# Moving the low parts of split weights from VectorE to GpSimd in a two-layer mLSTM/GLA decoder step

## The chip, the core and the metric

The kernel runs on one core of a Trainium2 chip. The metric is the device time of one execution in microseconds; the time before is the median of three runs. TensorE is the matmul engine, VectorE, ScalarE and GpSimd are the engines for elementwise work, SyncE issues the DMAs.

## The reference

1024 prompt tokens and 64 sample tokens (8 sequences of 8) go through two layers. Each layer is a token mixer (layer 0 an mLSTM, layer 1 gated linear attention, GLA) and a SwiGLU feed-forward, each between two RMS norms:

```
for i in range(2):
    h = rms_norm(x, g_pre_mix[i])
    mix = mlstm(h) if i == 0 else gla(h)        # in-projection, chunked recurrence, out-projection
    x = x + rms_norm(mix, g_post_mix[i])
    h = rms_norm(x, g_pre_ffn[i])
    h = (silu(h @ w_gate[i]) * (h @ w_up[i])) @ w_down[i]
    x = x + rms_norm(h, g_post_ffn[i])
```

D_MODEL is 1024, the feed-forward is 2816 wide, all data is fp32. The states of both mixers are outputs too.

## The kernel before, in words

Activations lie transposed, features on the 128 partitions and tokens along the columns, in two blocks: block 0 has 512 tokens, block 1 has 576, as two halves of 288.

**Split matmuls.** A product in fp32 is made of three products in the faster fp32r type. Every weight tile and every activation tile has a high part (its value in fp32r) and a low part (what is left), and TensorE adds low x high, high x high and high x low in PSUM (`products`, line 813).

**Units.** The work of TensorE on weights is a list of 396 units, each with one weight tile of 128 x 1024: P (a 128-column piece of an in-projection), W (out-projection), G and U (gate and up), D (two pieces of the down-projection, four groups of 128 outputs each). In the feed-forward they come as G D D U G U, over and over. A unit takes 24 matmuls of 512 columns in block 0 or 48 of 288 in block 1. The unit of number n uses slot n mod 3 of three buffers: `w_stage` (as loaded), `w_hi`, `w_lo`.

**Who makes what for unit n.** SyncE loads `w_stage` (line 567); it waits until the low part of the unit three before is made (semaphore `w_lo`). ScalarE makes `w_hi` by a copy that rounds (line 1079), after TensorE has left the slot. VectorE makes `w_lo = w_stage - w_hi` (`lo`, line 1363) after a wait on `w_hi`, and TensorE starts the unit after a wait on `w_lo`.

**Order.** Each engine runs the list of units in its own program, written out by loops: for unit n first the parts of unit n + 2 (ScalarE `hi`, VectorE `lo`), then its eviction, then the steps that tags have put beside that unit. VectorE puts `lo(n + 2)` ahead of the eviction, in a D unit between the first and the second group:

```
for q, grp in enumerate(u.groups):
    if q == 1 and n + 2 < len(units):
        lo(n + 2)
```

Evictions: a G tile is evicted by ScalarE (line 1132, `evicted`). A U tile is multiplied with it by VectorE (line 1391), ScalarE copies the product to `hid_hi` (line 1136), VectorE makes `hid_lo` (line 1394). A D group is copied to Y (line 1405, first pair) or added to it (line 1407) by VectorE; TensorE has four PSUM banks for all units and waits until a bank has been emptied.

**Steps beside the units.** A norm is a rstd (lines 1424 to 1429, after sums of squares, line 1374, and a matmul with a matrix of means, line 849), then the rows of the post norm, two to a unit (lines 1439 and 1442, then the squares), then the rows of the next pre norm (line 1458 for the value, ScalarE's high part, line 1454 for the low part). They stand beside units of the other block that are not D. The mixers' chunks of 128 tokens are spread over units in the same way; of the GLA's, `la1` and `la2` make exponents of seven levels (lines 1650, 1651) and the decayed keys (line 1691), for which TensorE waits at line 950.

GpSimd has four memsets of constants before the program, and no part in it.

Of the kernel before, what the change touches and what calls it, by code (L numbers as in the profile page):

```python
# [7 lines left out]
F32 = mybir.dt.float32  # L8
F32R = mybir.dt.float32r
U32 = mybir.dt.uint32  # L10
ALU = mybir.AluOpType
# [3 lines left out]
D = 1024  # L15
# [33 lines left out]
NW = 3  # L49
# [285 lines left out]
def wait(eng, sem, value):  # L335

    if value > 0:
        eng.wait_ge(sem, value)
# [131 lines left out]
def program(nc, g, plan, a):  # L470
    units, norms = plan.units, plan.norms
    s = {name: nc.alloc_semaphore(name) for name in SEMS}
# [13 lines left out]
    def grouped(ap, blk):  # L486
        return ap.rearrange("p (g t) -> p g t", g=NG[blk])

    def bank(b, blk):
        return ps[:, b:b + NG[blk], 0:GW[blk]]  # L490
# [51 lines left out]
    def unit(kind, layer, blk, i, j=0):  # L542
        return units[plan.at[kind, layer, blk, i, j]]

    rstds_before = {}
    n = 1
# [14 lines left out]
    with nc.Block() as block:  # L561
# [505 lines left out]
        def _(act):  # L1067
# [283 lines left out]
            for n, u in enumerate(units):  # L1351
# [3 lines left out]
                for t in u.tags:  # L1355
                    if t[0] in steps:
                        steps[t[0]](*t[1:])

        @block.vector
        def _(dve):  # L1360
            def lo(n):
                dve.wait_ge(s["w_hi"], n + 1)
                dve.tensor_tensor(g.wlo[:, n % NW, :], g.wst[:, n % NW, :], g.whi[:, n % NW, :].bitcast(F32),  # L1363
                                  ALU.subtract).then_inc(s["w_lo"], 1)

            def add_square(i, k, b):
                j = SUM(i, k)
                acc, sq = g.n.acc[:, 0:NT[b]], g.n.sq[:, j % 2, 0:NT[b]]
                dve.wait_ge(s["squared"], j + 1)
                if k == 0:  # L1370
                    dve.tensor_copy(acc, sq).then_inc(s["summed"], 1)
                else:
                    dve.wait_ge(s["summed"], j)
                    dve.tensor_tensor(acc, acc, sq, ALU.add).then_inc(s["summed"], 1)  # L1374

            def evict(n, u):
                b = u.blk
                if u.kind == "P" and u.i >= 17:
                    dve.wait_ge(s["left_act"], u.groups[0].ev)
                    E = g.E[:, u.slot, 0:NT[b]]  # L1380
                    j = V_HEAD[u.layer] + u.i - 17
                    dve.tensor_scalar(E, E, g.vec[:, j:j + 1], None, ALU.mult).then_inc(s["gained"], 1)
                elif u.kind == "W":
                    add_square(plan.norm[2 * u.layer, b].sum0, u.i, b)
                elif u.kind == "U":
                    grp = u.groups[0]
                    pr = g.E[:, 2, 0:NT[b]]
                    dve.wait_ge(s["groups"], grp.n + 1)
                    dve.wait_ge(s["left_act"], unit("G", u.layer, b, u.i).groups[0].ev)
                    wait(dve, s["hid_lo_ready"], u.hid - 1)  # L1390
                    dve.tensor_tensor(grouped(pr, b), bank(grp.bank, b), grouped(g.E[:, u.i % 2, 0:NT[b]], b), ALU.mult  # L1391
                                      ).then_inc(s["left_dve"], 1)
                    dve.wait_ge(s["hid_hi_ready"], u.hid)
                    dve.tensor_tensor(g.hl[:, u.i % 2, 0:NT[b]], pr, g.hh[:, u.i % 2, 0:NT[b]].bitcast(F32),  # L1394
                                      ALU.subtract).then_inc(s["hid_lo_ready"], 1)
                elif u.kind == "D":
                    N = plan.norm[2 * u.layer + 1, b]
                    for q, grp in enumerate(u.groups):
                        if q == 1 and n + 2 < len(units):
                            lo(n + 2)  # L1400
                        m = 4 * u.j + q
                        Y = grouped(g.Y[b][:, m, :], b)
                        dve.wait_ge(s["groups"], grp.n + 1)
                        if u.i == 0:
                            dve.tensor_copy(Y, bank(grp.bank, b)).then_inc(s["left_dve"], 1)
                        else:
                            dve.tensor_tensor(Y, bank(grp.bank, b), Y, ALU.add).then_inc(s["left_dve"], 1)  # L1407
                        if u.i == PAIRS - 1 and q:
                            add_square(N.sum0, m - 1, b)
                    if u.i == PAIRS - 1:  # L1410
                        add_square(N.sum0, 4 * u.j + 3, b)


            def sumx(n, k0, k1):
                for k in range(k0, k1):
                    add_square(norms[n].sum1, k, norms[n].blk)
# [413 lines left out]
                     "mg4": mgates, "ma": ma, "mb": mb, "md": md, "me": me, "lg": lgate, "la1": la1, "la2": la2, "la3": la3,  # L1830
                     "l1": l1, "l2": l2, "lb": lb, "le": le, "ss": ss, "sh": sh}
            dve.wait_ge(s["consts"], 16 * CONSTS)
            lo(0)
            sumx(0, 0, KD)
            lo(1)
            rstd(0, 1)
            pre(0, 0, KD)
            for n, u in enumerate(units):
                if u.kind != "D" and n + 2 < len(units):
                    lo(n + 2)  # L1840
                evict(n, u)
                for t in u.tags:
                    if t[0] in steps:
                        steps[t[0]](*t[1:])
# [93 lines left out]
```

## Time and profile before

| | |
|---|---|
| three runs | 2768.99, 2770.28, 2760.65 us; median 2768.99 us |
| the profiled execution | 2773.79 us, its span 2771.7 us |
| granted TensorE clock, mean | 0.986 |
| TensorE matmuls | 2652.2 us busy (96%), 16042 |
| VectorE | 1489.8 us busy (54%), 2286 instructions |
| ScalarE | 1020.4 us busy (37%), 1455 instructions |
| GpSimd | 0.2 us busy, 4 instructions |
| DMA | 331.25 MB, 120 GB/s |

The span is the time from the first to the last instruction of the profiled execution. The busy time of TensorE's matmuls comes from pipelined instructions with modelled ends, so that 96% busy does not mean 96% of its peak. An idle engine costs time only where another waits for it.

### The profile page before, as it was taken

The page shows a single profiled execution, that of the slowest core. Times are in us where ns is not written, and L with a number is a line of the kernel's source. Part 1 is how long each engine was busy: PE and PEld are TensorE (multiplying, and loading weights), DVE is VectorE, ACT ScalarE, POOL GpSimd, SP SyncE. Part 2 cuts the span into 40 slices and gives each one's busy share as a digit, 9 for nine tenths or more (in the row PEclk, how much of TensorE's full clock was granted, in tenths as well). Part 3 has the DMA queues.
Part 4 walks back from the last instruction along what each step waited for, and adds up shares of the span by engine and source line. Part 5 has one row for each costly group of instructions (what it writes and reads, how often), then busy time and mean ns, then how long its engine had stood idle before and what let it go on. Part 6 is the DMA issues. An engine that isn't in the chain of part 4 may idle for free.

```text
span 2771.7 us, 38345 instructions
## 1 busy us (share of the span) xinstructions
PE 2652.2 (96%) x16042; PEld 2392.2 (86%) x16042; DVE 1489.8 (54%) x2286; ACT 1020.4 (37%) x1455; POOL 0.2 (0%) x4
## 2 busy tenths in 40 slices
PE   5999999999999999999999999999999989999996
PEld 3889998877987998789999987998886979999996
DVE  4534455555367663356655676326766377444435
ACT  3443344542334332344433343325343243222222
POOL 0000000000000000000000000000000000000000
PEclk9999999999999999999999999999999999999998
DMA  4455445435323332442332333344225433322222
GB/s 159 140 162 156 129 144 157 132 114 173 126 84 127 106 120 100 153 146 74 106 104 69 115 110 121 125 134 139 90 91 182 133 110 126 111 83 85 77 84 84
DMA packets 181728, 331.25 MB, mean 120 GB/s; under 512 B 19477, under 2 KB 98965, under 8 KB 181557
## 3 DMA queue, kind: packets, MB, share of 16 engines
q1 hardware_dynamic: 181556, 328.81, 36.8%
q8 instruction: 127, 2.08, 0.3%
q14 instruction: 45, 0.36, 0.0%
HBM read 272.48 MB, written 56.28 MB: 119 GB/s over the span
## 4 chain that ended last, share of the span: by engine, by line
PE 83%; DVE 9%; ACT 4%; issue 2%; DMA 2%; SPq 0%; ACTq 0%; DVEq 0%
PE ps L813 75%; PE ps L967 2%; ACT w_hi L1079 1%; DMA w_stage<-w_down_in 1%; DVE Y L1439 1%; DVE n_xs L1442 1%; DVE w_lo L1363 1%; DVE evicted L1391 1%; ACT hid_hi L1136 1%; DVE n_normed L1458 1%; PE ps L908 1%; PE ps L901 1%; PE ps L1042 1%; PE ps L902 1%; PE ps L993 0%
## 5 line engine op out<-in xcount | busy, mean ns | idle before, releaser
L813 PE MATMUL ps<-HH,w_lo 128*128 128x288 f32 (+1 forms) x3696 | 1026.0, 332 | 10.1 <-DVE HL L1454 7.4
L813 PE MATMUL ps<-HH,w_hi 128*128 128x288 f32 (+1 forms) x3696 | 1012.1, 328 | 0.0
L813 PE MATMUL ps<-HL,w_hi 128*128 128x288 f32 (+1 forms) x3696 | 1012.1, 328 | 0.0
L813 PEld LDWEIGHTS ps<-HH,w_lo 128*128 128x128 f32 x3696 | 632.3, 189 | 74.3 <-issue 17.9
L1363 DVE TENSOR_TENSOR w_lo<-w_stage,w_hi 128x1024 fp32r<-128x1024 f32 x396 | 483.8, 1222 | 358.4 <-ACT w_hi L1079 357.5
L813 PEld LDWEIGHTS ps<-HL,w_hi 128*128 128x128 f32 x3696 | 631.1, 189 | 49.5
L813 PEld LDWEIGHTS ps<-HH,w_hi 128*128 128x128 f32 x3696 | 631.2, 189 | 47.3
L1079 ACT ACTIVATE w_hi<-w_stage 128x1024 fp32r<-128x1024 f32 x396 | 416.2, 1052 | 474.9 <-PE ps L813 347.4
L813 PE MATMUL ps<-hid_hi,w_lo 128*128 128x288 f32 (+1 forms) x1056 | 300.8, 340 | 37.9 <-DVE Y L1407 18.0
L1407 DVE TENSOR_TENSOR Y<-ps,Y 128x512 f32<-128x512 f32 (+1 forms) x320 | 227.5, 721 | 153.8 <-PE ps L813 153.0
L813 PE MATMUL ps<-hid_lo,w_hi 128*128 128x288 f32 (+1 forms) x1056 | 293.0, 332 | 0.0
L813 PE MATMUL ps<-hid_hi,w_hi 128*128 128x288 f32 (+1 forms) x1056 | 293.0, 332 | 0.0
L813 PEld LDWEIGHTS ps<-hid_hi,w_lo 128*128 128x128 f32 x1056 | 183.1, 193 | 64.8 <-issue 21.9
L1136 ACT ACTIVATE hid_hi<-evicted 128x512 fp32r<-128x512 f32 (+1 forms) x88 | 57.9, 658 | 430.2 <-DVE evicted L1391 430.2
L813 PEld LDWEIGHTS ps<-hid_lo,w_hi 128*128 128x128 f32 x1056 | 183.6, 193 | 15.0
L813 PEld LDWEIGHTS ps<-hid_hi,w_hi 128*128 128x128 f32 x1056 | 183.5, 193 | 13.5
L1391 DVE TENSOR_TENSOR evicted<-ps,evicted 128x512 f32<-128x512 f32 (+1 forms) x88 | 63.6, 723 | 209.5 <-PE ps L813 209.5
L1105 ACT ACTIVATE evicted<-ps 128x512 f32<-128x512 f32 (+1 forms) x96 | 59.9, 624 | 281.5 <-PE ps L813 281.4
L1374 DVE TENSOR_TENSOR n_sum<-n_sum,n_sq 128x512 f32<-128x512 f32 (+1 forms) x112 | 80.9, 723 | 99.7 <-ACT n_sq L1085 96.1
L1132 ACT ACTIVATE evicted<-ps 128x512 f32<-128x512 f32 (+1 forms) x88 | 54.8, 623 | 174.4 <-PE ps L813 174.1
L1394 DVE TENSOR_TENSOR hid_lo<-evicted,hid_hi 128x512 fp32r<-128x512 f32 (+1 forms) x88 | 63.9, 726 | 63.7 <-ACT hid_hi L1136 63.7
L1085 ACT ACTIVATE n_sq<-n_xs 128x512 f32<-128x512 f32 (+1 forms) x64 | 41.6, 657 | 70.5 <-DVE n_xs L1442 69.0
(191 smaller groups left out, 1618.2 us busy)
## 6 DMA issues: line engine op xcount, KB each, us to landing
w_stage<-w_in_in SPq DMA_DIRECT2D x100, 512.0 KB, 3.7
w_stage<-w_gate_in SPq DMA_DIRECT2D x88, 512.0 KB, 3.5
w_stage<-w_up_in SPq DMA_DIRECT2D x88, 512.0 KB, 3.6
w_stage<-w_down_in SPq DMA_DIRECT2D x88, 512.0 KB, 3.6
w_stage<-w_out_in SPq DMA_DIRECT2D x32, 512.0 KB, 4.1
proj_scratch<-evicted SPq DMA_DIRECT2D x48, 288.0 KB, 2.2
proj_scratch<-evicted SPq DMA_DIRECT2D x48, 256.0 KB, 2.1
x_scratch<-n_xs SPq DMA_DIRECT2D x3, 2304.0 KB, 9.3
```

The lines of the kernel that those rows point to most:

```text
L813: mm = pe.matmul(ps[:, grp.bank + t, 0:W], wsl(w, k), x[:, k, t * W:(t + 1) * W], start=(q == 0 and m == 0), stop=(q == len(ks) - 1 and m ...
L967: mm = pe.matmul(ps[0:n, M0 + b, at + h * m:at + (h + 1) * m], k, q, start=True, stop=True)
L1079: act.activation(g.whi[:, n % NW, :], g.wst[:, n % NW, :], ACT.Copy).then_inc(s["w_hi"], 1)
L1085: act.activation(grouped(dst, b) if src.shape != dst.shape else dst, src, ACT.Square).then_inc(s["squared"], 1)
L1105: act.activation(grouped(g.E[:, u.slot, 0:NT[b]], b), bank(grp.bank, b), func, scale=scale).then_inc(s["left_act"], 1)
L1132: act.activation(grouped(g.E[:, c, 0:NT[b]], b), bank(grp.bank, b), ACT.Silu).then_inc(s["left_act"], 1)
L1136: act.activation(g.hh[:, u.i % 2, 0:NT[b]], g.E[:, 2, 0:NT[b]], ACT.Copy).then_inc(s["hid_hi_ready"], 1)
L1363: dve.tensor_tensor(g.wlo[:, n % NW, :], g.wst[:, n % NW, :], g.whi[:, n % NW, :].bitcast(F32), ALU.subtract).then_inc(s["w_lo"], 1)
L1374: dve.tensor_tensor(acc, acc, sq, ALU.add).then_inc(s["summed"], 1)
L1391: dve.tensor_tensor(grouped(pr, b), bank(grp.bank, b), grouped(g.E[:, u.i % 2, 0:NT[b]], b), ALU.mult).then_inc(s["left_dve"], 1)
L1394: dve.tensor_tensor(g.hl[:, u.i % 2, 0:NT[b]], pr, g.hh[:, u.i % 2, 0:NT[b]].bitcast(F32), ALU.subtract).then_inc(s["hid_lo_ready"], 1)
L1407: dve.tensor_tensor(Y, bank(grp.bank, b), Y, ALU.add).then_inc(s["left_dve"], 1)
```

## The change

GpSimd gets a program of its own: for each unit in order, it waits for the unit's high part and makes its low part, with the same operands and the same semaphore. All calls of `lo` leave VectorE's program, and nothing else changes.

```diff
+        @block.gpsimd
+        def _(pool):
+            for n in range(len(units)):
+                pool.wait_ge(s["w_hi"], n + 1)
+                pool.tensor_tensor(g.wlo[:, n % NW, :], g.wst[:, n % NW, :], g.whi[:, n % NW, :].bitcast(F32),
+                                   ALU.subtract).then_inc(s["w_lo"], 1)
+
         @block.vector
         def _(dve):
-            def lo(n):
-                dve.wait_ge(s["w_hi"], n + 1)
-                dve.tensor_tensor(g.wlo[:, n % NW, :], g.wst[:, n % NW, :], g.whi[:, n % NW, :].bitcast(F32),
-                                  ALU.subtract).then_inc(s["w_lo"], 1)
-
...
                     for q, grp in enumerate(u.groups):
-                        if q == 1 and n + 2 < len(units):
-                            lo(n + 2)
                         m = 4 * u.j + q
...
             dve.wait_ge(s["consts"], 16 * CONSTS)
-            lo(0)
             sumx(0, 0, KD)
-            lo(1)
             rstd(0, 1)
             pre(0, 0, KD)
             for n, u in enumerate(units):
-                if u.kind != "D" and n + 2 < len(units):
-                    lo(n + 2)
                 evict(n, u)
```

VectorE's order before, in the feed-forward of layer 1 on block 0 with the post norm of block 1 beside it: an up unit, a gate unit and the first down unit (`w_lo` is the weights' low part, `hid_lo` the hidden tile's, `n_xs` the residual stream, `n_sum` the sum of squares):

```order
L1363 TENSOR_TENSOR w_lo<-w_stage,w_hi 128x1024
L1391 TENSOR_TENSOR evicted<-ps,evicted 128x512
L1394 TENSOR_TENSOR hid_lo<-evicted,hid_hi 128x512
L1439 SCALAR_TENSOR_TENSOR Y<-Y,vec,n_rstd 128x576
L1442 TENSOR_TENSOR n_xs<-n_xs,Y 128x576
L1439 SCALAR_TENSOR_TENSOR Y<-Y,vec,n_rstd 128x576
L1442 TENSOR_TENSOR n_xs<-n_xs,Y 128x576
L1374 TENSOR_TENSOR n_sum<-n_sum,n_sq 128x576 x2
L1363 TENSOR_TENSOR w_lo<-w_stage,w_hi 128x1024
L1439 SCALAR_TENSOR_TENSOR Y<-Y,vec,n_rstd 128x576
```

The ten rows hold two of `w_lo`, one ahead of each unit's other work. The same place now (lines after the change are shifted by up to two):

```order
L1393 TENSOR_TENSOR evicted<-ps,evicted 128x512
L1396 TENSOR_TENSOR hid_lo<-evicted,hid_hi 128x512
L1439 SCALAR_TENSOR_TENSOR Y<-Y,vec,n_rstd 128x576
L1442 TENSOR_TENSOR n_xs<-n_xs,Y 128x576
L1439 SCALAR_TENSOR_TENSOR Y<-Y,vec,n_rstd 128x576
L1442 TENSOR_TENSOR n_xs<-n_xs,Y 128x576
L1376 TENSOR_TENSOR n_sum<-n_sum,n_sq 128x576 x2
L1439 SCALAR_TENSOR_TENSOR Y<-Y,vec,n_rstd 128x576
```

The two rows of `w_lo` are gone, and the rest keeps its order. GpSimd's program before, which is constants and the barrier at the end:

```order
L1916 ISA
L1916 MEMSET const-float32-0.0 128x1
L1916 MEMSET const-float32-1.0 128x1
L1916 MEMSET const-bfloat16-1.0 128x1
L1916 MEMSET const-uint8-127 128x1
L1846 ISA
```

Nothing stands between the constants and the barrier. GpSimd's program now:

```order
L1912 MEMSET const-float32-1.0 128x1
L1912 MEMSET const-bfloat16-1.0 128x1
L1912 MEMSET const-uint8-127 128x1
L1359 UNCONDITIONAL_BRANCH
L1363 ISA
L1363 TENSOR_TENSOR w_lo<-w_stage,w_hi 128x1024 x396
L561 UNCONDITIONAL_BRANCH
L1842 ISA
```

All 396 low parts now stand there, one after the other, with nothing between them.

## Rows read from the trace of the kernel before

**Rows 1.** The page's part 1: busy time and share of each engine.

```profile
PE 2652.2 (96%) x16042; PEld 2392.2 (86%) x16042; DVE 1489.8 (54%) x2286; ACT 1020.4 (37%) x1455; POOL 0.2 (0%) x4
```

**Rows 2.** Waits: who waited for whom; us in total, times, longest us.

```profile
PE ps L813 <- DVE Y L1407: 18.0, 14, 3.7
PE ps L950 <- DVE l_k_decayed L1691: 9.4, 6, 2.4
PE ps L813 <- DVE Y L1405: 8.0, 3, 4.3
...
PE ps L813 <- ACT evicted L1132: 6.3, 8, 1.6
DVE w_lo L1363 <- ACT w_hi L1079: 357.5, 239, 16.6
```

**Rows 3.** Windows: stretch, length, busy us of PE, PEld, DVE, ACT, POOL, clock.

```profile
1580.00:1700.00 120.00, 110.84 (x574) 95.06 (x573) 82.33 (x106) 48.20 (x61) 0.00 (x0) 0.97 0.36 119
2380.00:2700.00 320.00, 320.00 (x2402) 320.00 (x2401) 132.62 (x148) 72.13 (x85) 0.00 (x0) 1.00 0.28 88
```

**Rows 4.** Timeline of DVE, 1637 to 1652 us: start, length, [idle before].

```profile
1637.06 1.23 DVE L1363 TENSOR_TENSOR w_lo<-w_stage,w_hi 128x1024 fp32r<-128x1024 f32 x1 [0.19 <-ACT w_hi L1079]
...
1639.58 0.69 DVE L1394 TENSOR_TENSOR hid_lo<-evicted,hid_hi 128x512 fp32r<-128x512 f32 x1 [0.70 <-ACT hid_hi L1136]
...
1643.23 1.61 DVE L1374 TENSOR_TENSOR n_sum<-n_sum,n_sq 128x576 f32<-128x576 f32 x2
1645.02 1.22 DVE L1363 TENSOR_TENSOR w_lo<-w_stage,w_hi 128x1024 fp32r<-128x1024 f32 x1 [0.17 <-ACT w_hi L1079]
1646.16 0.81 DVE L1439 SCALAR_TENSOR_TENSOR Y<-Y,vec,n_rstd 128x576 f32<-128x576 f32 x1
...
1650.74 0.68 DVE L1405 COPY Y<-ps 128x512 f32<-128x512 f32 x1
```

**Rows 5.** Timeline of PE: four of its waits for Y, one for keys.

```profile
953.70 0.85 PE L813 MATMUL ps<-hid_hi,w_lo 128*128 128x288 f32 x2 [3.25 <-DVE Y L1405]
...
1485.67 0.85 PE L813 MATMUL ps<-hid_hi,w_lo 128*128 128x288 f32 x2 [2.32 <-DVE Y L1407]
...
1651.57 0.77 PE L813 MATMUL ps<-hid_hi,w_lo 128*128 128x512 f32 x1 [4.29 <-DVE Y L1405]
...
1937.18 0.66 PE L950 MATMUL ps<-ident,l_k_decayed 128*128 128x128 f32 x4 [2.43 <-DVE l_k_decayed L1691]
...
2244.18 0.77 PE L813 MATMUL ps<-hid_hi,w_lo 128*128 128x512 f32 x1 [2.87 <-DVE Y L1407]
```

**Rows 6.** Groups by form: busy us, mean ns of one, idle before.

```profile
L1363 DVE TENSOR_TENSOR w_lo<-w_stage,w_hi 128x1024 fp32r<-128x1024 f32 x396 | 483.8, 1222 | 358.4 <-ACT w_hi L1079 357.5
...
L1374 DVE TENSOR_TENSOR n_sum<-n_sum,n_sq 128x576 f32<-128x576 f32 x56 | 42.4, 756 | 67.2 <-ACT n_sq L1085 65.7
...
L1382 DVE TENSOR_SCALAR evicted<-evicted,vec 128x576 f32<-128x576 f32 x16 | 8.3, 521 | 34.8 <-ACT evicted L1105 34.7
...
L1504 DVE TENSOR_TENSOR_SCAN Y<-Y,m_before 4x512 f32<-4x512 f32 x1 | 1.3, 1272 | 0.0
```

**Rows 7.** Timeline of DVE in the steady feed-forward, 2502 to 2509 us.

```profile
2502.39 0.76 DVE L1394 TENSOR_TENSOR hid_lo<-evicted,hid_hi 128x576 fp32r<-128x576 f32 x1 [0.75 <-ACT hid_hi L1136]
2503.34 1.23 DVE L1363 TENSOR_TENSOR w_lo<-w_stage,w_hi 128x1024 fp32r<-128x1024 f32 x1 [0.19 <-ACT w_hi L1079]
```

**Rows 8.** Timeline of all engines at the start, 16 to 24 us.

```profile
16.56 1.23 DVE L1363 TENSOR_TENSOR w_lo<-w_stage,w_hi 128x1024 fp32r<-128x1024 f32 x1 [16.56 <-ACT w_hi L1079]
17.70 0.42 DVE L1371 COPY n_sum<-n_sq 128x512 f32<-128x512 f32 x1
...
23.84 2.05 PE L849 MATMUL ps<-n_sum,avg 128*128 128x512 f32 x2 [23.84 <-DVE n_sum L1374]
```

**Rows 9.** Timeline of DVE in a GLA chunk, 1930 to 1934 us.

```profile
1930.95 1.23 DVE L1363 TENSOR_TENSOR w_lo<-w_stage,w_hi 128x1024 fp32r<-128x1024 f32 x1 [1.72 <-ACT w_hi L1079]
...
1933.48 0.69 DVE L1394 TENSOR_TENSOR hid_lo<-evicted,hid_hi 128x512 fp32r<-128x512 f32 x1 [0.70 <-ACT hid_hi L1136]
```

## The prediction

> **What bounds the kernel now.** I read the page's busy shares first. TensorE is busy 96% of the span, VectorE 54%, ScalarE 37%, and GpSimd does 0.2 us in all [rows 1]. So the program is a stream of matmuls, and VectorE can only matter where TensorE waits for it. The waits of TensorE by releaser come next [rows 2]: 18.0 us in 14 waits for the add of a down-projection group to Y (line 1407), 8.0 us in 3 for the copy that stands there in the first pair (line 1405), 6.3 us in 8 for ScalarE's eviction of a gate tile, 9.4 us in 6 for the decayed keys of the GLA layer. That is 41.7 us, 1.5% of the span: all that a lighter VectorE could win beside the start.
>
> The stages show where it lies. From 2380 to 2700 us TensorE has no idle time at all, with VectorE busy 132.62 of 320 us. From 1580 to 1700 us, a norm beside the feed-forward, VectorE is busy 82.33 of 120 us and TensorE only 110.84 [rows 3]. The timeline of VectorE before one wait there shows the chain [rows 4]: low part (1637.06), eviction of the up tile, low part of the hidden tile (1639.58), two rows of the norm with their squares, a second low part (1645.02), two more rows, and only at 1650.74 the copy that empties the bank for which TensorE waits. TensorE goes on at 1651.57 after 4.29 us [rows 5]. In the rest of this text a **place** is such a spot: an up unit and a gate unit full of norm work, then a down unit. There are nine among the 17 waits for Y; four of the others are in the GLA chunks, and the wait of 2.32 us at 1485.67 has the rstd ahead of it and no low part [rows 5].
>
> **The change, step by step.**
>
> 1. VectorE loses 396 instructions of 1222 ns, 483.8 us, and GpSimd gets them [rows 6]. VectorE's 1489.8 us should become 1006 us. TensorE, ScalarE and SyncE run the same instructions in the same order. VectorE also no longer stands in its own order until ScalarE has made a high part (357.5 us of waiting before the low parts [rows 2]); most of that only becomes waiting for something else.
>
> 2. The price of one low part on GpSimd. No row shows GpSimd at elementwise work: four memsets in 0.2 us are all it has [rows 1]. The low bound is VectorE's own 1.22 us. The high bound is the slowest rate of a row over many columns, the scan of 4x512 at 1272 ns: twice that for 1024 columns, 2.54 us [rows 6]. I take 2.5 us, the costly end, because VectorE's 1222 ns is one column per step with nothing to spare, and an engine that did it as fast would be a gift that nothing here shows. The Trainium skill ("GPSIMD Engine Reference", section 3.1) gives 4497 ns for a two-input tensor_tensor of 2048 fp32 columns; half of it is an estimate of 2.25 us, and at that price the sum below would be 2.5 us smaller. No row here shows it.
>
> 3. Is it in time? ScalarE makes the high part of a unit at the start of the unit two before it, and TensorE needs the low part two units later. A unit of block 1 is 48 matmuls, 6.4 us (320 us for 2402 matmuls [rows 3]); one of block 0 has 512 columns for 576, so at the same rate some 5.7 us. 2.5 us fit into two units, 11 to 13 us. The load of the weights three units on waits for the low part as well; that becomes at most 1.3 us later, and has a unit of room. I cost this at nothing; the cover is gone if the price goes above a unit, 5.7 us, since then GpSimd falls behind the stream.
>
> 4. The steady feed-forward. The low part of the hidden tile starts at 2502.39 and ends at 2503.1, the weights' low part starts at 2503.34 [rows 7]. On GpSimd this would run from 2503.3 to 2505.8, when VectorE has nothing to do. Its next work is adds from PSUM. Cost nothing; nothing to gain either, for TensorE does not wait.
>
> 5. Both engines at SBUF together. This is the unknown that decides. No row of before shows it. The bounds: they don't disturb each other (0), or a VectorE instruction with two SBUF inputs stands still until a running GpSimd instruction has ended (up to the whole 2.5 us). What the rows show: TENSOR_SCALAR with one SBUF input does 576 columns in 521 ns, a third faster than the two-input row (756 ns) [rows 6]. So VectorE has two ways into SBUF, uses both for one input when it can, and needs both for two inputs. Whoever joins has to take one away. I take the standing still as likeliest and keep the 0 as a rival.
>
> With that, a place changes so. First low part: before, from its start to the start of the hidden tile's low part there are 1639.58 - 1637.06 = 2.52 us. Now the eviction (one input from PSUM) and ScalarE's copy run beside GpSimd, and the hidden tile's low part, with two SBUF inputs, starts when GpSimd ends, after 2.5 us: **0**. Second low part: before, it and its wait took from 1644.84 (end of the squares) to 1646.16, 1.3 us. Now all that VectorE has there are two-input instructions, so GpSimd's 2.5 us are inserted whole: **+1.2 us**. The add or copy of Y comes 1.2 us later, and TensorE, which already waits there, waits 1.2 us more. Nine places: **+10.8 us**. Inside the down units the adds have one SBUF input and no low part among them any more; TensorE did not wait for that, so 0.
>
> 6. The start. The low part of unit 0 stands ahead of the sum of squares, 16.56 to 17.70 [rows 8], and the chain to the first matmul (after 23.84 us of idle) goes through it. On GpSimd it holds the adds 2.5 instead of 1.14 us: **+1.4 us**.
>
> 7. GLA chunks. VectorE sits idle 1.72 us for the high part, makes the low part at 1930.95 and the hidden one at 1933.48 [rows 9]: 2.53 us, the same pattern as in a place. With GpSimd in the way the hidden one starts at 1933.45: 0. The waits for the keys (2.43 us at 1937.18) stay.
>
> **The sum.** 10.8 + 1.4 = +12.2 us on the profiled execution's own 2773.8 us: 2786.0. That execution lies 4.8 us above the median of the three runs, 2769.0, so the forecast is 2769.0 + 12.2 = **2781.2 us**. About 0.5% (14 us) is what a measurement of this kernel can tell from no change, so this reads as "the same, on the slow side": 484 us leave the second busiest engine, and nothing is won.
>
> **The rivals.**
>
> A. *They don't disturb each other.* Then each place wins both low parts, up to 2.4 us, as far as TensorE waits there, and the GLA chunks win the wait for the high part too: ScalarE's copy of the hidden tile follows the high part at 1930.9, and the hidden low part starts at about 1931.6, 1.9 us earlier [rows 9]. Of the 41.7 us there remain what the long waits have above 2.4 (3.25, 3.7, 4.3 and 2.87 [rows 2, 5]: 4.4 us), the 2.32 us at 1485.67, and 0.5 us at three waits for the keys: 8.2. Gain 33.5 us, **2735.5 us**. For it: the argument of step 5 only says that a path is shared, not that it is held for a whole instruction. The Trainium skill ("SBUF - State Buffer", section "Who interferes with whom") speaks for my forecast and against this rival: a VectorE instruction with two SBUF inputs contends with a GpSimd instruction that reads SBUF, and one of them blocks fully. No row of this trace can show it.
>
> B. *They exclude each other, but VectorE keeps its turn through a row of back-to-back instructions*, and GpSimd gets in at its pauses. Then a second low part costs VectorE nothing: -1.2 us at each of nine places, about -10 us, **2759 us**. Against it: between two-input instructions of rows 4 there are small gaps, and a waiting engine needs one.
>
> C. *GpSimd's instruction is long enough to pass the cover: slower.* It decides from 2.52 us on, where the eviction and ScalarE's copy of an up unit no longer hide it. At three times VectorE's price, 3.7 us, a place loses 1.2 us at the first and 2.4 us at the second low part, nine times 3.6 = 32.4; the start 2.6 (3.7 less 1.14); the keys of the six GLA waits 1.2 each, 7.2. Together +42 us, **2811 us**. For it: a programmed engine, and GpSimd may itself be held by VectorE in turn. Against: the steady stretch would still be free of it, up to 5.7 us.
>
> D. *It is hidden anyway* is part of the forecast: at VectorE's own price under exclusion the places give -0.1 us each, about 2768 us.
>
> **How the numbers follow.** Forecast 0.45, with its own range 2768 to 2789 (price from 1.22 to 2.54 us, and some us for down units that are just in time today): 0.27 of it within 0.5%, 0.18 slower. A 0.33: 0.31 faster, 0.02 within. B 0.07: 0.03 faster, 0.04 within. C 0.15, slower. Faster 0.34, same 0.33, slower 0.33. Both signs hold much, so the range reaches from A to C, 2736 to 2812; outside are the far ends of both.
>
> **What the new profile would show.** GpSimd with 396 instructions, spaced by a unit, of about 2.5 us. The steady stretch still without idle time of TensorE (if not, step 3 or 4 is wrong). Two-input VectorE instructions of norm work with a mean above today's 756 ns, up to 3 us in single ones, while the adds from PSUM keep 756 ns: that is step 5; unchanged means say A. The wait at the place of 1651 us near 5.5 us for the forecast, 1.9 for A, near 3 for B. The chain for the keys at 2.4 us unchanged, gone or nearly so under A. The forecast is wrong in size if places are more than the nine, that is if down units that were in time today begin to wait, and wrong in kind if TensorE waits for low parts directly.

## The result and the profile after

| | before | after |
|---|---|---|
| median | 2765.97 us (4 runs, 2760.65 to 2770.28) | 2791.14 us (4 runs, 2786.70 to 2792.32) |
| ratio | | 1.0085, 95% interval 1.0062 to 1.0108 |
| profiled execution, its span | 2773.79, 2771.7 us | 2790.17, 2788.1 us |
| sum of TensorE's waits | 99.3 us | 115.5 us |

The kernel became slower by 25.2 us by the medians and by 16.4 us between the two profiled executions: the one of before lies 7.8 us above its median. By the interval of the ratio the loss is 17 to 30 us, so the profiled pair shows the low end of it. What the traces are compared for is the 16.4. The forecast was 2781.2 us, from a sum of +12.2 us.

The page's part 1 after the change, against [rows 1]:

```profile
PE 2652.3 (95%) x16042; PEld 2390.0 (86%) x16042; DVE 1218.5 (44%) x1890; ACT 1018.6 (37%) x1455; POOL 973.4 (35%) x400
```

TensorE computes as long as before (2652.2 us), so all of the loss is waiting. VectorE lost 396 instructions of 1222 ns, which should have left 1006.0 us, and it shows 1218.5: 212 us in which its other instructions last longer than they did. The waits of TensorE by releaser (us in total, times, longest), against [rows 2]:

```profile
PE ps L849 <- DVE n_sum L1376: 29.7, 5, 24.1
PE ps L813 <- DVE Y L1407: 24.6, 15, 4.3
PE ps L813 <- DVE Y L1405: 10.0, 3, 5.1
PE ps L950 <- DVE l_k_decayed L1691: 8.4, 7, 2.2
PE ps L813 <- POOL w_lo L1363: 7.5, 5, 2.1
...
PE ps L813 <- ACT evicted L1132: 5.8, 8, 1.4
...
PE ps L1033 <- DVE l_q_batch L1779: 2.6, 2, 1.8
```

All rows of this view together, before and after, give a ledger that closes: 115.5 - 99.3 = 16.2 of the 16.4 us. The waits for Y went from 18.0 + 8.0 to 24.6 + 10.0, **+8.6 us**. TensorE waits for low parts themselves for 7.5 us, where before one wait of 0.6 us went to VectorE's: **+6.9 us**. Of these, 2.4 us are two waits (1693.05 and 2293.24 us) at spots where TensorE of before waited 1.57 and 1.47 us as well, in the row "issue"; new are 0.8 us at the start (1.39 for 0.56) and 3.7 us near 425 and 433 us, **+4.5 us**. The other rows give the remaining 0.7: the first sums of squares +0.9, rows of the mixers and the sample steps +4.4 in all (2.5 of them four waits for `l_y_normed`, below), that issue row -3.1, the decayed keys -1.0, ScalarE's evictions -0.5.

Which VectorE instructions last longer? The groups by form (busy us, mean ns of one, idle before):

```profile
L1363 POOL TENSOR_TENSOR w_lo<-w_stage,w_hi 128x1024 fp32r<-128x1024 f32 x396 | 973.2, 2460 | 1770.7 <-ACT w_hi L1079 1770.7
...
L1407 DVE TENSOR_TENSOR Y<-ps,Y 128x576 f32<-128x576 f32 x160 | 120.3, 756 | 171.6 <-PE ps L813 171.5
L1458 DVE SCALAR_TENSOR_TENSOR n_normed<-n_xs,vec,n_rstd 128x576 f32<-128x576 f32 x32 | 41.8, 1346 | 0.1
L1396 DVE TENSOR_TENSOR hid_lo<-evicted,hid_hi 128x576 fp32r<-128x576 f32 x44 | 41.7, 947 | 34.9 <-ACT hid_hi L1136 34.9
L1384 DVE TENSOR_SCALAR evicted<-evicted,vec 128x576 f32<-128x576 f32 x16 | 18.1, 1139 | 86.9 <-ACT evicted L1105 86.9
L1746 DVE TENSOR_SCALAR small<-small 128x4 f32<-128x4 f32 x8 | 18.3, 2284 | 0.0
```

The add with one input from PSUM keeps its 756 ns. The two-input instructions of the same width, 758 and 813 ns in the trace of before, take 947 (hid_lo) and 1346 (n_normed). But the TENSOR_SCALAR with a single SBUF input, 521 ns before [rows 6], has more than doubled, and an instruction on four columns, 162 ns in the trace of before, takes 2284 ns: it stands still for nearly a whole low part. The timeline of GpSimd, VectorE and TensorE at the place of [rows 4]:

```profile
1645.29 2.40 POOL L1363 TENSOR_TENSOR w_lo<-w_stage,w_hi 128x1024 fp32r<-128x1024 f32 x1 [5.53 <-ACT w_hi L1079]
...
1646.35 1.88 DVE L1396 TENSOR_TENSOR hid_lo<-evicted,hid_hi 128x512 fp32r<-128x512 f32 x1 [0.70 <-ACT hid_hi L1136]
...
1653.02 2.76 POOL L1363 TENSOR_TENSOR w_lo<-w_stage,w_hi 128x1024 fp32r<-128x1024 f32 x1 [5.33 <-ACT w_hi L1079]
1653.57 2.82 DVE L1442 TENSOR_TENSOR n_xs<-n_xs,Y 128x576 f32<-128x576 f32 x1
...
1660.19 0.76 PE L813 MATMUL ps<-hid_hi,w_lo 128*128 128x512 f32 x1 [5.06 <-DVE Y L1405]
```

GpSimd's first low part runs until 1647.69; the hidden tile's, of 0.69 us, starts at 1646.35 and ends at 1648.23, half a microsecond after it. GpSimd's second one covers the n_xs of 0.76 us, which takes 2.82. TensorE's wait is 5.06 us where it was 4.29 [rows 5]. GpSimd's second low part itself takes 2.76 us, where the median is 2.40.

**The second source** is in the in-projections of layer 0 on block 1, where the norm of block 0 stands beside them. The timeline before of VectorE, ScalarE's high parts and SyncE's queue (SPq: what it issued):

```profile
395.42 0.52 DVE L1382 TENSOR_SCALAR evicted<-evicted,vec 128x576 f32<-128x576 f32 x1 [0.23 <-ACT evicted L1105]
...
398.75 0.38 SPq L592 DMA_DIRECT2D x_scratch<-n_xs  x1
399.17 0.58 SPq L567 DMA_DIRECT2D w_stage<-w_in_in  x1
...
408.48 1.06 ACT L1079 ACTIVATE w_hi<-w_stage 128x1024 fp32r<-128x1024 f32 x1 [4.02 <-DMA w_stage<-w_in_in]
```

and the same after, until TensorE waits:

```profile
396.55 2.07 DVE L1384 TENSOR_SCALAR evicted<-evicted,vec 128x576 f32<-128x576 f32 x1 [0.93 <-ACT evicted L1105]
...
401.42 0.38 SPq L592 DMA_DIRECT2D x_scratch<-n_xs  x1
401.84 0.58 SPq L567 DMA_DIRECT2D w_stage<-w_in_in  x1
...
412.61 1.06 ACT L1079 ACTIVATE w_hi<-w_stage 128x1024 fp32r<-128x1024 f32 x1 [6.40 <-DMA w_stage<-w_in_in]
...
422.37 2.36 POOL L1363 TENSOR_TENSOR w_lo<-w_stage,w_hi 128x1024 fp32r<-128x1024 f32 x1 [6.24 <-ACT w_hi L1079]
422.86 2.18 DVE L1384 TENSOR_SCALAR evicted<-evicted,vec 128x576 f32<-128x576 f32 x1 [0.80 <-ACT evicted L1105]
...
424.78 0.54 PE L813 MATMUL ps<-HH,w_lo 128*128 128x288 f32 x2 [1.63 <-POOL w_lo L1363]
...
429.85 1.04 ACT L1079 ACTIVATE w_hi<-w_stage 128x1024 fp32r<-128x1024 f32 x1
...
433.37 0.50 PE L813 MATMUL ps<-HH,w_lo 128*128 128x512 f32 x1 [2.07 <-POOL w_lo L1363]
```

VectorE's scaling of an evicted row (line 1384) takes 2.07 us for 0.52, and the norm rows behind it come later. SyncE's store of the residual stream (2048 KB, line 592) waits for the last of them, and a weight load is queued behind the store: 401.84 for 399.17. Of these 2.67 us the whole stream was 1.13 late already (the scaling starts at 396.55 for 395.42), and the stop gives 1.55. The load then landed after 10.75 us where it took 9.28 before, and the high part starts 4.1 us later. The longer flight isn't put down to GpSimd: with VectorE making the low parts there, three runs below (the last two and the one without the 102 low parts) have flights of 10.9 to 11.1 us too, and each of them waits 0.84 to 0.88 us for a low part near 426 us. From here on each unit waits for the last by way of three engines: a low part stops the scaling (2.18 us at 422.86), behind it come the rows of the next norm, ScalarE's copies of them, and then the next high part (429.85). From one high part to the next it is 8.6 us where it was 7.5. So TensorE waits 1.63 us for a low part and then 2.07 us more. No wait of more than 0.6 us for a low part stood in the trace before.

**Where the time goes.** The same matmuls can be laid side by side in both traces. Those of 390 to 440 us before take 6.6 us longer after the change: 4.3 us of it is waiting, and most of the rest is TensorE at the lower of its two clock levels, which was granted for 3.4 us after the wait at 433.37. The other big step is in the GLA chunks and sample steps of layer 1 (stretch, length, busy us of PE, PEld, VectorE, ScalarE, GpSimd, then the granted clock, in two views, before and after):

```profile
1900.00:2160.00 260.00, 247.41 (x1315) 202.30 (x1313) 174.48 (x362) 105.64 (x171) 0.00 (x0) 0.99 0.38 122
...
1908.00:2177.00 269.00, 251.90 (x1315) 203.77 (x1315) 170.01 (x333) 105.57 (x171) 78.31 (x30) 0.97 0.38 118
```

That is 9.0 us more for the same 1315 matmuls, half of it waiting, half TensorE longer busy at a mean granted clock of 0.97 for 0.99. In each of the four chunks there the TENSOR_SCALAR on four columns (line 1746) stands still, and TensorE waits 0.64 us for `l_y_normed` behind it, which it did not before. The rest of the program gains and loses in turn and adds about 1 us. In the trace before, TensorE stood at the lower level about as long (79.9 us in all, 75.5 after), in other spots, so in sum only the waits remain.

### The profile page after: what moved, and what is told of

The parts are those of the page before. It is cut to its first block, busy times and chain, and to the rows that moved or that the text cites. A ratio compares the mean times of both kernels' runs of the same rounds, so it can differ in the third digit from the quotient of the medians.

```text
span 2788.1 us, 38342 instructions
## 1 busy us (share of the span) xinstructions
PE 2652.3 (95%) x16042; PEld 2390.0 (86%) x16042; DVE 1218.5 (44%) x1890; ACT 1018.6 (37%) x1455; POOL 973.4 (35%) x400
## 4 chain that ended last, share of the span: by engine, by line
PE 80%; DVE 11%; ACT 4%; issue 2%; DMA 2%; SPq 1%; POOL 0%; DVEq 0%; ACTq 0%
PE ps L813 72%; PE ps L967 2%; DVE n_xs L1442 1%; DVE n_normed L1458 1%; DVE Y L1439 1%; DMA w_stage<-w_down_in 1%; DMA w_stage<-w_in_in 1%; DVE hid_lo L1396 1%; ACT hid_hi L1136 1%; DVE HL L1454 1%; DVE n_sum L1376 1%; ACT w_hi L1079 1%; PE ps L1042 1%; PE ps L901 1%; PE ps L902 1%
## 5 line engine op out<-in xcount | busy, mean ns | idle before, releaser
L1363 POOL TENSOR_TENSOR w_lo<-w_stage,w_hi 128x1024 fp32r<-128x1024 f32 x396 | 973.2, 2460 | 1770.7 <-ACT w_hi L1079 1770.7
L813 PE MATMUL ps<-hid_hi,w_lo 128*128 128x288 f32 (+1 forms) x1056 | 298.6, 337 | 45.2 <-DVE Y L1407 24.6
L1376 DVE TENSOR_TENSOR n_sum<-n_sum,n_sq 128x512 f32<-128x512 f32 (+1 forms) x112 | 89.6, 800 | 156.3 <-ACT n_sq L1085 152.7
L1396 DVE TENSOR_TENSOR hid_lo<-evicted,hid_hi 128x512 fp32r<-128x512 f32 (+1 forms) x88 | 87.9, 999 | 74.2 <-ACT hid_hi L1136 74.2
L1384 DVE TENSOR_SCALAR evicted<-evicted,vec 128x512 f32<-128x512 f32 (+1 forms) x32 | 28.6, 896 | 190.0 <-ACT evicted L1105 190.0
```

The source lines that it names most:

```text
L813: mm = pe.matmul(ps[:, grp.bank + t, 0:W], wsl(w, k), x[:, k, t * W:(t + 1) * W], start=(q == 0 and m == 0), stop=(q == len(ks) - 1 and m ...
L1363: pool.tensor_tensor(g.wlo[:, n % NW, :], g.wst[:, n % NW, :], g.whi[:, n % NW, :].bitcast(F32), ALU.subtract).then_inc(s["w_lo"], 1)
```

## The experiments

The theory: a VectorE instruction that uses GpSimd's way into SBUF stands still until GpSimd's instruction ends. What decides is then either the length of one such stop and where it falls, or the total time for which GpSimd holds the way. The rivals: what matters is only that low parts come later (price, not disturbance); or that GpSimd's writing is in the way. Ratios are to the kernel before on the same chip, with 95% intervals; they lie up to 0.001 beside the quotient of the medians.

**Reading alone and writing alone.** Both are the kernel before, with VectorE still making all low parts. In the first GpSimd subtracts constants beside it:

```diff
+            for n in range(len(units)):
+                pool.wait_ge(s["w_hi"], n + 1)
+                for r in range(4):
+                    wait(pool, s["scratched"], 4 * n + r)
+                    pool.tensor_tensor(g.scr[:, :], g.lmask[:, 0:256].bitcast(F32), g.lmask[:, 256:512].bitcast(F32),
+                                       ALU.subtract).then_inc(s["scratched"], 1)
```

> VectorE keeps the low parts and the kernel is the one before, but beside each high part GpSimd runs four subtractions of 256 columns from constants in SBUF to a scratch tile that nobody reads: the reads of the changed kernel, with no product that anyone waits for. Theory (the engines exclude each other while both read SBUF with two inputs): two-input VectorE instructions of norm work are held, among them now the low parts themselves, so each of the nine places loses about 2.5 us at the second low part and some of it at the first; slower than before by 25 to 60 us. Rival (only the later low part costs, not the shared path): within 3 us of before, and no VectorE group has a higher mean.

Measured: 2873.56 us against 2767.82, ratio 1.038 (1.0366 to 1.0395). In the second the four subtractions are eight memsets of the same scratch tile:

> As the run with reads, but GpSimd writes zeros to the scratch tile eight times per unit and reads nothing. Theory (reading is what excludes): two-input VectorE instructions keep their means (756 ns for 576 columns); only one-input ones in their fast form (line 1382, the copies of line 1779) may be held; within 6 us of before. Rival (any instruction of GpSimd holds VectorE): as slow as the run with reads, 25 us or more.

Measured: 2767.26 us, ratio 0.9994 (0.9982 to 1.0006). The page's part 1 and groups by form of the reads:

```profile
PE 2683.4 (93%) x16042; PEld 2414.8 (84%) x16042; DVE 1707.1 (59%) x2286; ACT 1020.2 (36%) x1455; POOL 1589.4 (55%) x1588
...
L1367 POOL TENSOR_TENSOR scratch_pool<-level_masks 128x256 f32<-128x256 f32 x1584 | 1589.2, 1003 | 1240.1 <-ACT w_hi L1080 1134.5 <-POOL scratch_pool L1367 0.4
```

and of the writes:

```profile
PE 2644.8 (96%) x16042; PEld 2384.7 (86%) x16042; DVE 1490.9 (54%) x2286; ACT 1020.7 (37%) x1455; POOL 995.0 (36%) x3172
...
L1366 POOL MEMSET scratch_pool<- 128x256 f32 x3168 | 994.8, 314 | 1724.8 <-ACT w_hi L1080 1562.6
L1391 DVE TENSOR_SCALAR evicted<-evicted,vec 128x576 f32<-128x576 f32 x16 | 9.0, 560 | 34.6 <-ACT evicted L1106 34.5
```

995 us of writing leave VectorE at 1490.9 us, 1.1 more than before, and the time where it was; 1589 us of reading add 217 us to VectorE and 105 us to the time. So it is reading that excludes, at least reading with two inputs, the only kind that was run. The writes do touch the one-input form a little (560 ns for 521). The loss of the reads was far above what was expected. Its waits are 68 us more than before and its matmuls are 31 us longer busy; the mean granted clock was 0.972 for 0.986. VectorE's own low parts went on needing GpSimd's way in here, so both engines held each other: GpSimd's mean is 1003 ns, where the pieces of 256 columns below have 799; the medians, 742 and 737 ns, agree.

**Lateness alone.** The kernel before, where GpSimd passes on the signal of a low part after four memsets of 64 columns, 0.84 us later in the median:

```diff
+                pool.wait_ge(s["w_lo_dve"], n + 1)
+                for r in range(4):
+                    wait(pool, s["scratched"], 3 * n + min(r, 3))
+                    ins = pool.memset(g.scr[:, 64 * r:64 * r + 64], 0.0)
+                    ins.then_inc(s["scratched" if r < 3 else "w_lo"], 1)
...
-                                  ALU.subtract).then_inc(s["w_lo"], 1)
+                                  ALU.subtract).then_inc(s["w_lo_dve"], 1)
```

> VectorE makes the low parts as before, but the semaphore for which TensorE and the loads wait is raised by GpSimd, after four small writes of zeros (64 columns each), about 1 us later: the lateness of the changed kernel's low parts without its reads. Theory: TensorE's direct waits for a low part around 424 and 433 us and the start of the second unit appear in part, 2 to 7 us; the places stay at 4.3 us at 1651 us. Rival (lateness is the whole loss): 20 us or more slower than before.

Measured: 2771.43 us, ratio 1.001 (0.9999 to 1.002), TensorE's waits 99.4 us. A low part that is 0.84 us late adds no waiting, and at most some 5 us by the interval. In the changed kernel it is ready 1.2 us later (2.47 us after the high part in the median, for 1.26). So lateness of that kind alone is not likely to have made 25 us, though this run has only two thirds of it.

**The length of one stop.** The changed kernel, with the low part in pieces of 512, 256 and 128 columns. The work of GpSimd grows, each single stop of VectorE shrinks:

```diff
-                pool.tensor_tensor(g.wlo[:, n % NW, :], g.wst[:, n % NW, :], g.whi[:, n % NW, :].bitcast(F32),
-                                   ALU.subtract).then_inc(s["w_lo"], 1)
+                for c in range(0, 1024, 256):
+                    ins = pool.tensor_tensor(g.wlo[:, n % NW, c:c + 256], g.wst[:, n % NW, c:c + 256],
+                                             g.whi[:, n % NW, c:c + 256].bitcast(F32), ALU.subtract)
+                ins.then_inc(s["w_lo"], 1)
```

> The changed kernel with each low part as two GpSimd instructions of 512 columns. Theory: the time for which the path is held is the same, in two pieces of about 1.25 us; VectorE may slip in between, so a single held instruction lasts at most about 2 us instead of 3, and the time is within 6 us of the changed kernel, 15 to 30 us above before. Rival (the length of a single hold decides): the loss falls by half or more, to within 10 us of before.

> The changed kernel with each low part as four GpSimd instructions of 256 columns. If the length of a single hold decides (halves lost 12 us where the whole lost 25), VectorE's instructions now get in after at most about 0.7 us and the loss shrinks again: 0 to 8 us above before, with the low part taking longer, 2.8 to 4 us. If it is the total time for which the path is held, the loss stays at the 12 us of the halves or grows with the sum of the pieces: 12 to 20 us.

> The changed kernel with each low part in eight pieces of 128 columns, which by the medians of the pieces (2397, 1292 and 737 ns) should take about 0.46 us each, 3.7 us together. If only the single hold counts, the series 25, 12, 0 us goes on below zero, 3 to 8 us faster than before. If the total of 3.7 us and the later low part now weigh more, it turns back: 0 to 10 us slower than before, with more waiting of TensorE for the low parts themselves than the 11 us of the quarters.

Measured, with the waits of TensorE read from the same view as above (for Y, lines with COPY and add together; for low parts; all rows):

| piece, columns | median ns of one | ratio (95%) | waits for Y | for low parts | all waits |
|---|---|---|---|---|---|
| none (before) | | 1 | 26.0 | 0.6 | 99.3 |
| 1024 (the change) | 2397 | 1.0085 (1.0062 to 1.0108) | 34.6 | 7.5 | 115.5 |
| 512 | 1292 | 1.0043 (1.0031 to 1.0055) | 30.3 | 7.2 | 105.8 |
| 256 | 737 | 0.9995 (0.9984 to 1.0005) | 21.8 | 11.4 | 97.7 |
| 128 | 460 | 1.0022 (1.0009 to 1.0035) | 17.0 | 21.1 | 100.8 |

The rows of the eighths for low parts and for Y:

```profile
PE ps L813 <- POOL w_lo L1364: 21.1, 9, 4.8
PE ps L813 <- DVE Y L1409: 14.2, 9, 3.0
...
PE ps L813 <- DVE Y L1407: 2.8, 2, 2.6
```

For the halves I had expected the loss to stay, 15 to 30 us above before; it was 12.4 us by the medians, so it is the length of one stop that counts, not the total. Two terms run against each other. With shorter stops the waits for Y fall steadily, to 9 us below those before. But a whole low part takes longer (eight pieces 3.7 us at their median, one 2.4), and TensorE waits for low parts directly, three times as long as with one piece. The quarters have the least in sum.

**Which low parts cost.** Four kernels with whole pieces. Which engine makes the low part of unit n depends on the kind of unit beside which it is made, n - 2; the two engines have semaphores of their own:

```diff
+    for n, u in enumerate(units):
+        u.maker = "w_lo_pool" if n >= 2 and units[n - 2].kind == "D" else "w_lo"
...
+                if n >= NW:
+                    sp.wait_ge(s[units[n - NW].maker], units[n - NW].made)
...
+                pe.wait_ge(s[u.maker], u.made)
```

The condition is the only line that differs among them. First the 86 beside D units on GpSimd, and then all but these:

> GpSimd makes only those low parts that VectorE made inside down units (a third of those in the feed-forward), VectorE the others, with a semaphore for each. Beside them VectorE works on adds with one input from PSUM. Theory of exclusion by the second SBUF input: nothing is held, nothing waited for this low part, within 4 us of before. Rival (any low part on GpSimd costs by being later and longer): about its share of the changed kernel's 25 us, 8 us or more.

> The complement: GpSimd makes all low parts but those inside down units. Theory: the whole loss of the changed kernel is here, 20 to 30 us above before, and a place like the one at 1651 us waits 5 us or more. Rival: two thirds of the loss, about 17 us, with the rest in the other run.

Measured: 2771.22 us, 1.001 (0.9998 to 1.0022), for the 86, and 2793.70 us, 1.0085 (1.0071 to 1.0099), for the other 310. Beside most D units VectorE's work is adds from PSUM, and they aren't held; by the times the loss lies outside. The trace of the first run is less clean:

```profile
PE ps L820 <- DVE Y L1424: 23.2, 17, 4.1
```

With the other row (7.6) the waits for Y are 30.8 us for 26.0: the wait at 1485.67 of [rows 5] is 4.06 for 2.32, since a down unit's low part holds the last step of a rstd (2.43 us for 0.69), and in GLA chunks between 1230 and 1402 us there are four more of some 0.67 us, behind an exponent step with two SBUF inputs that is held (2.58 us for 0.42). So these 86 are cheap, not free, and the run can't tell a cost of up to 6 us from none. Then the 102 beside in-projections (with the first two), once on VectorE and once alone on GpSimd:

> The changed kernel with the 102 low parts that come beside in-projection units (and the first two) back on VectorE; the other 294 stay whole on GpSimd. Theory (a second source of loss, apart from the places: in the in-projections a store waits for a held one-input instruction, and the weight loads queue behind it): some 7 to 10 us of the loss go away, +13 to +18 us against before, a ratio of 1.005 to 1.0065, and the two direct waits of TensorE for low parts at 424.78 and 433.37 us are gone. Rival (the loss lies in the places and the GLA chunks, and the start costs a microsecond or two): the loss stays nearly whole, +21 to +25 us, 1.0075 to 1.009.

> The complement: GpSimd makes only the 102 low parts beside in-projection units (and the first two), VectorE the other 294. Theory: +6 to +10 us against before, 1.002 to 1.0035, with the direct waits near 425 and 433 us as in the changed kernel; together with its complement the two losses make the whole one. Rival: +1 to +3 us, 1.0005 to 1.001. If the two losses add to clearly less than the whole, the places of one kind also delay the other.

Measured: 2778.58 us, 1.0039 (1.0025 to 1.0054), without them, and 2776.86 us, 1.0033 (1.0021 to 1.0046), with them alone. TensorE's waits of the first:

```profile
PE ps L820 <- DVE Y L1424: 24.4, 15, 4.3
PE ps L820 <- DVE Y L1422: 10.0, 3, 5.0
...
PE ps L820 <- POOL w_lo L1371: 2.5, 2, 1.3
```

and of the second:

```profile
PE ps L820 <- DVE Y L1424: 18.1, 14, 3.7
PE ps L820 <- DVE Y L1422: 8.1, 3, 4.3
...
PE ps L820 <- POOL w_lo L1371: 5.2, 3, 1.9
```

The waits split cleanly. Without the 102 the waits for Y are those of the changed kernel; with them alone, those of before, and the waits for low parts are there (1.74 and 1.94 us at 422.49 and 431.09). Two separate losses of 0.39% and 0.33%, and their sum, 0.72%, is that of the change within its interval; by the medians they are 9.4 and 7.6 us. The first run came out below its expected 13 to 18 us, so the places and the GLA chunks cost a little less than I had made of it. What the runs show is that the 102 cost something of their own. By which chain is read from the timelines alone: no run kept the low parts on GpSimd and took the store, or the scaling, out of the way.

**Two versions that are faster.** The kernel before, with VectorE's low parts moved out of the chain instead of to another engine: beside an up unit with norm rows behind the rows' evictions, beside a gate unit into the D units that follow.

```diff
+            def rows_beside(n):
+                return n + 2 < len(units) and any(t[0] in ("post", "pre") for t in units[n].tags)
+            def deferred(n):
+                return units[n].kind == "G" and units[n + 1].kind == "D" and rows_beside(n)
...
+                        if q == 2 and deferred(n - 1):
+                            lo(n + 1)
-                        if q == 1 and n + 2 < len(units):
+                        if q == (3 if deferred(n - 1) else 1) and n + 2 < len(units):
```

> The kernel before, all low parts on VectorE, but in up and gate units with norm rows beside them the low part is taken out of the chain: in an up unit it stands between the eviction and the hidden tile's low part, where VectorE idles 0.7 us for ScalarE, in a gate unit ahead of a down unit it waits until that down unit's second add. If the chain of VectorE before the first add of Y is what TensorE waits for at the nine places, each gives back 0.7 and 1.2 us where it waits that long: 10 to 17 us faster than before. If not, within 3 us of before.

Measured: 2762.89 us against 2768.62, ratio 0.9974 (0.9962 to 0.9985): 7 us, under the expected 10 to 17. The waits for Y fell from 26.0 to 12.3 us, but TensorE now waits for the low parts that were pushed back:

```profile
PE ps L813 <- DVE w_lo L1363: 13.2, 6, 3.5
PE ps L813 <- DVE Y L1418: 10.2, 9, 2.3
```

The other takes what the runs had shown: quarters on GpSimd, but whole on VectorE beside in-projections, where the stops fall ahead of a store and on the way to the next high part.

> GpSimd makes the low parts in four pieces of 256 columns, but not those that VectorE made inside the in-projection units; these stay whole on VectorE. Against before, the run with quarters everywhere had lost 7 us by the end of the first layer's in-projections (waits for late low parts around 424 us) and won 14 us after them. If the two are separable, only the gain stays: 8 to 15 us faster than before. If the loss at the projections comes from the start and the norm and not from the low parts there, 0 to 4 us faster.

Measured: 2759.24 us (12 runs) against 2768.11, ratio 0.9977 (0.9967 to 0.9988), below both kernels. Its rows:

```profile
PE ps L820 <- DVE Y L1426: 12.8, 6, 4.1
PE ps L820 <- DVE Y L1424: 9.0, 3, 4.6
...
PE ps L820 <- POOL w_lo L1372: 5.2, 2, 2.8
```

All its waits are 91.2 us, 8.1 less than before. 8.9 us are gained by the medians, within the expected 8 to 15, and some 6 by the ratio, below it. The intervals of the two faster versions overlap (0.9962 to 0.9985 and 0.9967 to 0.9988): no run shows that GpSimd is worth more here than a better order on VectorE. It has the waits for Y of the quarters (21.8 us) and 4.8 us less of waiting for low parts of either engine (6.6 for 11.4).

## Why the prediction was right or wrong

The forecast, "the same, on the slow side", had the side right, and exclusion, the mechanism of step 5, held; the size did not: +16.4 us between the profiled executions for +12.2 forecast, and +25.2 by the medians. 2791.1 lies within the range but outside the forecast's own (2768 to 2789). The range reached from A to C, 76 us, and chances were split in thirds over faster, same and slower, so that being within it says little. The sum also came nearer than its terms: the places and the start were put too high, and two terms that were put at nothing were not nothing.

- Step 1, the move: right in count. VectorE's 1006 us became 1218.5, since the forecast left the stops out of its busy time.
- Step 2, the price: right, and by luck. 2.5 us was twice a scan of VectorE, the costly end of two bounds, and neither says anything of GpSimd; measured 2.46 in the mean and 2.40 in the median. The estimate of 2.25 us from the Trainium skill ("GPSIMD Engine Reference", section 3.1) was 6% too low against the median.
- Step 3, "cost nothing": **the step that failed**. It asked whether GpSimd's own 2.4 us fit into two units, which they do. It did not ask what the stopped VectorE instructions hold up on the loading side: the norm rows, the store that waits for them and the load queued behind it, and ScalarE's next high part. New direct waits for low parts came to +4.5 us where 0 stood. The prediction had named such waits as what would make it wrong in kind. The run with the 102 low parts alone gave +0.33%, 7.6 us by the medians, from this side alone.
- Step 4, the steady feed-forward: right, TensorE has no wait there.
- Step 5, exclusion: right in kind, with every mark it named (two-input instructions longer, adds from PSUM at 756 ns). Its list was too short. It reasoned that a one-input TENSOR_SCALAR at 521 ns for 576 columns uses both ways into SBUF when it can, and then counted only two-input instructions as held. By its own reasoning the fast one-input forms had to be held too: 1139 ns in the mean, 2284 ns for four columns. The stops behind both terms that were put at nothing, steps 3 and 7, are of such instructions: the scaling of line 1384, the four columns of line 1746, the copy of line 1779. The Trainium skill ("SBUF — State Buffer", section "Who interferes with whom") says so as well: `copy` and `tensor_scalar` can enter a mode that takes the shared pair and then contend with GpSimd, who issues first blocks the other fully. The trace agrees (521 to 1139 ns); it was this sentence that the prediction passed over.
- The places: +1.2 us at each of nine, 10.8 in all, were forecast; all waits for Y gave +8.6. The named place gave +0.77 (4.29 to 5.06): `n_xs` starts 0.55 us into the second low part, so that the stop costs 2.06 us and not 2.5, less the 1.3 that left. The wait at 953.70 of [rows 5] went from 3.25 to 3.85, the one at 2244.18 from 2.87 to 3.85. The wait at 1485.67, counted as no place for want of a low part ahead of it, grew most, from 2.32 to 4.06: the last step of the rstd ahead of it is held, 2.43 us for 0.69. And down units that were in time began to wait, which the prediction had named as what would make it wrong in size: 1.86 us at 786.34, 0.58 and 0.47 behind it, for one of 1.56 before.
- Step 6, the start: +1.4 forecast, +0.27 measured (23.84 to 24.11).
- Step 7, the GLA chunks: the chain for the keys was right (9.4 us before, 8.4 after), but the chunks are not free: four waits of 0.64 us for `l_y_normed` are new, and with the sample steps the stretch from 1900 to 2160 us takes 9.0 us longer. In the sample steps:

```profile
2114.19 2.37 POOL L1363 TENSOR_TENSOR w_lo<-w_stage,w_hi 128x1024 fp32r<-128x1024 f32 x1 [5.28 <-ACT w_hi L1079]
2114.27 2.31 DVE L1779 COPY l_q_batch<-l_q_decayed 128x16 f32<-128x16 f32 x1
...
2116.73 0.63 PE L1033 MATMUL ps<-l_sample_state,l_q_batch 128*32 128x256 f32 x4 [1.79 <-DVE l_q_batch L1779]
```

A copy of 16 columns, 162 ns otherwise, stands behind a low part of 2.37 us, and TensorE waits 1.79 us (timeline of the kernel after). A wait of 1.4 us for the same step of the mLSTM, which the trace before had, is gone, so the waits of the two together grew by 0.4 us.

Of the rivals, A (no disturbance, 2735.5 us) and B (VectorE keeps its turn, 2759) are excluded by the groups above. C's condition was not needed: the price stayed under its 2.52 us in the mean, though single low parts took up to 4.49 us, and the result lies between forecast and C by another way. In A, the four long waits have 4.5 us above 2.4, not 4.4. What remains open: the medians differ by 8.8 us more than the profiled pair, and only the pair has been taken apart. The ledger of waits stands for one execution of each.

## What to carry to other kernels

Before work is moved to GpSimd, list what VectorE runs meanwhile and which of it the exclusion holds: not by size, for a copy of 16 columns waits for a whole instruction like one of 576, but by whether it reads SBUF with two inputs or in the fast one-input form. Then ask what hangs on each held instruction on the other side too, stores and the loads queued behind them, and the work of a third engine. If the move is wanted, cut GpSimd's work into pieces, since the single stop decides (here 256 columns were the least of the two costs), and keep it away from spots where a short VectorE instruction stands on a chain. And try first to move the work within VectorE's own program: that gained as much here.

## What was not expected of the hardware

GpSimd at this subtraction takes about 0.19 us and 2.16 ns a column by the medians of 1024, 512, 256 and 128 columns (2397, 1292, 737, 460 ns): the four lie on this line within 10 ns. It needs 1.96 times VectorE's 1222 ns, so that moving the work costs twice the time and stops VectorE for nearly half of what it saved: 484 us left, 212 came back as stops. Memsets of GpSimd, 995 us of them, cost VectorE 1.1 us.
